# A streaming encoder layer with 16,384 product-key experts: sixteen more tokens by gathered rows, two gate blocks kept on chip

## The chip, the cores and the metric

The kernel runs on one core of one Trainium2 chip. Its time is the device time of one launch in microseconds, with the inputs in HBM. The core has five engines with instruction streams of their own: PE (TensorE, matmuls), DVE (VectorE), ACT (ScalarE), POOL (GpSimd) and SP (SyncE, which only issues DMAs here). They are ordered against one another by semaphores alone, which the kernel writes out by hand.

## The reference

One layer over 576 tokens (512 of a prompt, 64 of a decode step) with 1,024 channels: three attention-like branches, a merge, and then the part that the change touches, a feed-forward of single-neuron experts. For each token and each of 8 heads the 16 best of 16,384 experts are found by product keys (2 x 128 sub-keys); an expert is one row of `u` and one row of `v`, 1,024 numbers each.

```python
def peer_block(tok, wq, keys, u, v):
    qr = (tok @ wq).reshape(p, PEER_HEADS, 2, PEER_DQ // 2)
    s = jnp.einsum('phcd,hckd->phck', qr, keys)
    top_s, top_i = lax.top_k(s, PEER_TOPK)
    cand = top_s[:, :, 0, :, None] + top_s[:, :, 1, None, :]
    ...
    g = jax.nn.softmax(best, axis=-1)
    act = jax.nn.gelu(jnp.einsum('phkd,pd->phk', u[eidx], tok))
    return jnp.einsum('phk,phkd->pd', (g * act), v[eidx])
```

So each token needs 8 x 16 = 128 rows of `u` (a dot product with the token, then GELU), 128 shares `g`, and the sum of 128 rows of `v`, weighted by share times GELU. After that come the residual add and a final RMSNorm.

## The kernel before

**Two ways for the experts.** The last 128 tokens (`NSP`) go by gathered rows: partition p holds token p, POOL fetches for each of `NST` = 128 expert slots the 128 rows that the tokens need (one indirect DMA of 512 KB, `fetch`, L526), and DVE makes a dot product with the token (`dot`, L1408) or adds the weighted row to `accS` (`combine`, L1505). The first 448 tokens (`TD`) go densely: all 16,384 experts are computed for all of them, as `NCH` = 128 chunks of 128 experts, in two phases.

**Phase U.** For each chunk, PE multiplies the chunk of `u` with the tokens: 8 blocks of channels, each in three bf16 products (high x high, high x low, low x high), 24 matmuls of 448 columns (`chunk`, in `tile`, L1569). The weights come from HBM as f32 (SP, 512 KB, 4 buffers `raw`), ACT makes the high half (L581, a ring of 8) and POOL the low half (L493). ACT applies GELU into `hb` (2 buffers, L903) and stores it in HBM as `hd` (L906). Chunks are run in bodies of 8. Bodies 0 to 5 run beside DVE's search for the best experts (`top16`, `pairs_of`), during which DVE also makes the first 8 dot products: the first two stand between the second and third of five search parts. When the search is done ACT makes the exponentials (L944, ahead of chunk 40), DVE normalises them, makes 16 more dot products, and PE turns the triples (first key, second key, share).

**Gate steps.** In bodies 6 to 13 each chunk but the first of a body is followed by a gate step (`g_step`, L1930 and L1931): DVE makes one-hots of the two keys for 8 tokens (`one_hots`, L1470 to L1474, double-buffered), PE multiplies them (16 matmuls of 128 columns), and ACT copies the result, the share of each of the 16,384 experts for these 8 tokens, into `gsb` (L927). Seven steps are a block of 56 tokens (`TBLK`); two blocks fit `gsb`, and each is written to HBM as `gd` in 8 pieces (`write_piece`, L912) while the next is made. DVE makes 1.5 dot products a step. Bodies 14 and 15 have chunks only.

**Phase V.** For each chunk SP loads 4 chunks' gates `Gb` and activations `Hb` (896 KB each, double-buffered groups) and the chunk of `v`; DVE multiplies them into `wb` (L1519), ACT takes the high half `W_hi` (L954), DVE the low one (L1510) and also the low half of the `v` chunk (`unit_low`, L1486), and adds one gathered row slot (`combine`, L1505). PE makes 24 matmuls of 448 columns into the 8 banks of PSUM (`peer_v`, L1978; the last four chunks by channel block, L1997). Then the residual, the squares and the final norm. A phase V chunk starts on PE only when all GELUs (`gelu_done`), all dot products and its `W_lo` are done.

The order of each engine is that of its program. The ones that matter in what follows, for DVE in phase V:

```python
for c in range(NCH):
    # every 4th chunk: wait for Gb and Hb
    wb = Hb * Gb            # L1519
    unit_low(c + 2)         # L1486
    w_low(c - 1)            # L1510
    combine(c)              # L1505
```

and for ACT at the end of phase U, where `FIRST_W` is {5: (0,), 6: (1,), 7: (2, 3)}:

```python
for k in range(BODY):
    chunk(J_END + 1, k)     # GELU of this chunk, high half of the unit 8 ahead, store
    for c in FIRST_W.get(k, ()):
        w_high(c, c)        # waits for wb of chunk c
```

## Time and profile before

| what | value |
|---|---|
| time, median of 3 runs | 2072.77 us (2071.75 to 2074.18) |
| the profiled execution's own time | 2072.76 us |
| its span in the trace | 2071.0 us |
| mean granted TensorE clock | 0.988 of full |
| PE, DVE, ACT, POOL busy | 96%, 69%, 41%, 39% of the span |
| DMA | 467.12 MB, 226 GB/s over the span |
| phase U on PE | from about 826 to 1466 us |
| phase V on PE | from 1470 to about 2055 us |

The span is what the trace covers; the launch adds 1.8 us to it. A matmul's duration in the trace is from its start to the end of its pipeline, so two in a row overlap; what counts is the distance of their starts. A row of idle time in brackets says how long an engine stood still before an instruction and what released it.

### The profile page before, as it was taken

How to read it: one execution, taken by the hardware profiler on the slowest of the kernel's cores; microseconds unless marked ns; L12 is line 12 of the kernel's file. 1: busy time of each engine (PE TensorE's matmuls, PEld its weight loads, DVE VectorE, ACT ScalarE, POOL GpSimd, SP SyncE). 2: the span in 40 equal slices, each digit the busy share in tenths (PEclk: the TensorE clock that was granted, in tenths of full speed). 3: DMA queues.
4: the chain of work that ended last, by engine and by line, in shares of the span. 5: the costliest groups of instructions: out<-in, count | busy, mean ns of one | idle time of the engine just before them, and what ended most of it. 6: DMA issues, size and time to landing. Idle time of an engine off the chain costs nothing.

```text
span 2071.0 us, 34453 instructions
## 1 busy us (share of the span) xinstructions
PE 1997.3 (96%) x12670; PEld 1226.8 (59%) x12680; DVE 1434.0 (69%) x2704; ACT 841.4 (41%) x1253; POOL 807.7 (39%) x514
## 2 busy tenths in 40 slices
PE   7799998999999999999999999999999999999997
PEld 6546666677777777555555555555455555555554
DVE  7743645433345566989889898984788777777774
ACT  6324334344443433333346556653333333333331
POOL 2532211211233354565676667666332222222210
PEclk9899999999999999999999999999999999999998
DMA  5732112222344322466689999999999888899871
GB/s 190 183 107 85 51 41 86 75 70 80 137 143 130 102 73 72 161 214 215 234 320 322 357 355 359 356 353 400 384 362 371 330 329 327 329 342 340 328 264 46
DMA packets 180321, 467.12 MB, mean 226 GB/s; under 512 B 18600, under 2 KB 85168, under 8 KB 179448
## 3 DMA queue, kind: packets, MB, share of 16 engines
q1 hardware_dynamic: 102304, 248.84, 34.8%
q0 software_dynamic: 36864, 134.23, 17.5%
q10 hardware_dynamic: 41048, 82.66, 10.8%
q8 instruction: 64, 1.05, 0.2%
q14 instruction: 41, 0.34, 0.0%
HBM read 393.54 MB, written 72.14 MB: 225 GB/s over the span
## 4 chain that ended last, share of the span: by engine, by line
PE 81%; DVE 9%; DMA 4%; issue 2%; ACT 2%; POOL 1%; ACTq 0%; SPq 0%; DVEq 0%; POOLq 0%
PE ps L1569 29%; PE ps L1978 27%; PE ps L1661 10%; PE ps L1585 3%; PE ps L1808 2%; PE ps L1930 1%; POOL w_lo L493 1%; PE ps L1931 1%; DMA rows<-in_u_rows,rowi 1%; DVE rows L1408 1%; PE ps L1997 1%; DMA hd<-hb 1%; PE ps L1773 1%; PE ps L1788 1%; DMA raw<-in_units 1%
## 5 line engine op out<-in xcount | busy, mean ns | idle before, releaser
L493 POOL TENSOR_TENSOR w_lo<-raw,w_hi 128x1024 bf16<-128x1024 f32 x225 | 499.6, 2222 | 756.5 <-ACT w_hi L581 731.7
L581 ACT ACTIVATE w_hi<-raw 128x1024 bf16<-128x1024 f32 x357 | 374.9, 1052 | 481.0 <-PE ps L1978 302.0
L1569 PE MATMUL ps<-act_hi,w_hi 128*128 128x448 bf16 (+1 forms) x1040 | 364.1, 351 | 1.1 <-DVE proj L1034 0.7
L1569 PE MATMUL ps<-act_hi,w_lo 128*128 128x448 bf16 (+1 forms) x1040 | 364.2, 351 | 0.0
L1569 PE MATMUL ps<-act_lo,w_hi 128*128 128x448 bf16 (+1 forms) x1040 | 364.1, 351 | 0.0
L1978 PE MATMUL ps<-W_hi,w_hi 128*128 128x448 bf16 x992 | 350.7, 354 | 4.0 <-DVE W_lo L1510 4.0
L1978 PE MATMUL ps<-W_lo,w_hi 128*128 128x448 bf16 x992 | 350.6, 353 | 0.0
L1978 PE MATMUL ps<-W_hi,w_lo 128*128 128x448 bf16 x992 | 350.5, 353 | 0.0
L526 POOL DMA_INDIRECT rows<-in_v_units,rowi x128 | 149.4, 1167 | 415.2 <-DVE accS L1505 398.4
L1486 DVE TENSOR_TENSOR w_lo<-raw,w_hi 128x1024 bf16<-128x1024 f32 x128 | 156.6, 1223 | 116.6 <-ACT w_hi L581 116.6
L903 ACT ACTIVATE hb<-ps 128x448 f32<-128x448 f32 x128 | 69.7, 545 | 325.1 <-PE ps L1569 300.2
L1408 DVE CUSTOM_DVE_ANT_0 rows<-rows,ps 128x1024 f32<-128x1024 f32 x128 | 153.2, 1212 | 60.6 <-DMA rows<-in_u_rows,rowi 60.3
L1661 PE MATMUL ps<-act_hi,w_hi 128*128 128x288 bf16 x640 | 185.1, 289 | 7.5 <-ACT wk L712 3.5
L1661 PE MATMUL ps<-act_lo,w_hi 128*128 128x288 bf16 x640 | 185.0, 289 | 0.0
L1661 PE MATMUL ps<-act_hi,w_lo 128*128 128x288 bf16 x640 | 184.9, 289 | 0.0
L1505 DVE SCALAR_TENSOR_TENSOR accS<-rows,wsp,accS 128x1024 f32<-128x1024 f32 x128 | 163.5, 1277 | 0.0
L1569 PEld LDWEIGHTS ps<-act_hi,w_lo 128*128 128x128 bf16 x1040 | 101.7, 98 | 94.0
L1569 PEld LDWEIGHTS ps<-act_hi,w_hi 128*128 128x128 bf16 x1040 | 101.5, 98 | 90.4 <-issue 1.2
L1569 PEld LDWEIGHTS ps<-act_lo,w_hi 128*128 128x128 bf16 x1040 | 101.6, 98 | 88.4
L1978 PEld LDWEIGHTS ps<-W_hi,w_hi 128*128 128x128 bf16 x992 | 97.3, 98 | 95.5 <-issue 5.3
L1978 PEld LDWEIGHTS ps<-W_hi,w_lo 128*128 128x128 bf16 x992 | 97.3, 98 | 91.3 <-issue 1.1
L1978 PEld LDWEIGHTS ps<-W_lo,w_hi 128*128 128x128 bf16 x992 | 97.3, 98 | 91.0 <-issue 0.9
(374 smaller groups left out, 3323.2 us busy)
## 6 DMA issues: line engine op xcount, KB each, us to landing
raw<-in_u_units SPq DMA_DIRECT2D x128, 512.0 KB, 5.0
raw<-in_v_units SPq DMA_DIRECT2D x128, 512.0 KB, 9.4
raw<-in_units SPq DMA_DIRECT2D x100, 512.0 KB, 3.3
hd<-hb ACTq DMA_DIRECT2D x128, 224.0 KB, 5.4
...
```

The lines of the kernel that those rows point to most:

```text
L493: pool.tensor_tensor(w_lo[:, k % RING, :], raw[:, k % RAW, :], w_hi[:, k % RING, :], ALU.subtract).then_inc(lo_ready, 1)
L526: pool.indirect_dma_start(out=rows[:, s % RG, :], out_offset=None, in_=table, in_offset=bass.IndirectOffsetOnAxis(ap=rowi[:, s:s + 1], axi ...
L581: act.activation(w_hi[:, k % RING, :], raw[:, k % RAW, :], ACT.Copy).then_inc(hi_ready, 1)
L903: act.activation(hb[:, k % 2, :], ps[:, k % 2, 0:TD], ACT.Gelu_apprx_tanh).then_inc(gelu_done, 1)
L1408: dve.tensor_tensor_reduce(out=rows[:, s % RG, :], in0=rows[:, s % RG, :], in1=tok, scale=1.0, scalar=0.0, op0=ALU.mult, op1=ALU.add, accu ...
L1486: dve.tensor_tensor(w_lo[:, (U_V + c) % RING, :], raw[:, (U_V + c) % RAW, :], w_hi[:, (U_V + c) % RING, :], ALU.subtract).then_inc(lo_read ...
L1505: dve.scalar_tensor_tensor(out=accS[:, :], in0=rows[:, s % RG, :], scalar=wsp[:, s:s + 1], in1=accS[:, :], op0=ALU.mult, op1=ALU.add).then ...
L1569: last = pe.matmul(ps[:, bank + half, 0:n], w[:, slot, col:col + P], x(k)[:, half * n:(half + 1) * n], start=(k == 0 and w is w_hi and x i ...
L1585: last = pe.matmul(ps[0:nf, bank, :], x[:, k, f0:f0 + nf], w[:, n % RING, k2 * 512:(k2 + 1) * 512], start=(k == 0 and x is hi and w is w_h ...
L1661: last = pe.matmul(ps[:, 6 + half, 0:HALF], w[:, n % RING, k * P:(k + 1) * P], x[:, k, half * HALF:(half + 1) * HALF], start=(m == 0), sto ...
L1808: last = pe.matmul(ps[r0:r0 + rows, 4 + x % 2, 0:n], v, wk[0:ns, 2 + i % 2, b * P:b * P + n], start=(b == 0), stop=(b == len(blocks) - 1))
L1978: ins = pe.matmul(ps[:, d, 0:TD], w[:, slot, d * P:(d + 1) * P], x[:, k, :], start=(first and w is w_hi and x is W_hi), stop=False)
```

## The change

- **Tokens.** 16 of the 448 dense tokens (`NX`) leave the two dense phases: `TDX` = 432 columns a matmul, GELU on 432. They go by rows too. As they fill only 16 partitions, their 128 experts each are spread over 8 groups of 16 partitions: 16 slots, each an indirect DMA of 128 rows. Their gates are still made with the others (the gate steps and `W_hi`, `W_lo`, `wb` stay at 448 columns; the tail of `hb` is filled once).
- **Their token.** ACT copies the 16 tokens eight times over (`x_rep`), PE turns this in 8 transposes behind the first body, ACT copies it back from PSUM. Their row numbers and shares (`xpair`) are moved to the 8 groups by 8 small DMAs that POOL issues with chunks 100 to 107.
- **Their rows.** In phase V, DVE makes 16 more dot products (`x_dot`, behind chunks 4, 6, ... 34) and 16 more weighted additions (`x_combine`, behind chunks 72, 74, ... 102) into `accX`; ACT makes one small GELU ahead of chunk 64. POOL fetches in that order: 32 more indirect DMAs. At the end PE adds up the 8 groups by 8 small matmuls with `sel`, and DVE adds the result.
- **Gates.** Only 6 of the 8 blocks of gates are written to HBM and read back (`NBK`); the last two stay in `gsb`, and DVE's product is made by two instructions, one from `Gb`, one from `gsb`. Bodies 13 and 14 have no stores of gates.
- **Activations.** `hd` is laid out by groups of 4 chunks, so that a group's load has 7,168 bytes in a row for each partition, not 4 times 1,792.
- **Places.** As `gsb` is kept, `W_hi`, `W_lo`, `Gb0`, `Hb0` and `wb` lie where the tables of the gate steps were; `Gb1`, `Hb1` and `accS` lie in `act_hi` and `act_lo`, which PE reads until the end of phase U. So the load of group 1 and DVE's first `combine` wait for the last matmul of phase U (`unit_used, U_V`), and the load of group 0 for the last gate step. `accS` is no longer cleared: the first `combine` writes it.

```diff
@@ SP
             for b in range(2):
-                sp.wait_ge(b_written[b], NBLK // 2 * PIECES * 16)
+                sp.wait_ge(b_written[b], NBK // 2 * PIECES * 16)
+            sp.wait_ge(b_evac, N_STEP)
             for b in range(2):
                 sp.wait_ge(h_written[b], 8 * (NCH - 2 * GRP))
             load_gh(0, 0, None)
             for k in range(GRP, 2 * GRP):
                 load(a["v_units"][k], (U_V + k) % RAW, False, U_V + k - RAW + 1)
+            sp.wait_ge(unit_used, U_V)
             load_gh(1, 1, None)
@@ POOL
+                if LOADS_X <= c < LOADS_X + 2 * N_XG:
+                    half, g = divmod(c - LOADS_X, N_XG)
+                    pool.wait_ge(x_known, 2)
+                    at, to = half * HP + HP - NX, half * HP + g * NX
+                    pool.dma_start(xin[to:to + NX, :, :], xpair[at:at + NX, :, g * NX:(g + 1) * NX]).then_inc(x_moved, 16)
...
+            for c in range(NCH):
+                fetch_v(n_main(c), v_rows, rowi[:, c:c + 1])
+                i = (c - X_DOT) // 2
+                if c == X_DOT + 2 * i and 0 <= i < NX:
+                    fetch_v(n_dot(i), a["u_rows"], rowx[:, i:i + 1])
+                i = (c - X_COMB) // 2
+                if c == X_COMB + 2 * i and 0 <= i < NX:
+                    fetch_v(n_comb(i), v_rows, rowx[:, i:i + 1])
@@ ACT
-                        if b == 1:
+                        if b == 1 and not last:
                             write_piece(it * 2, 0, k, it * (2 * G_BODY) + G_BODY)
-                        elif not first:
+                        if b == 0 and not first:
                             write_piece(it * 2 - 1, 1, k, it * (2 * G_BODY))
...
             for k in range(BODY):
                 chunk(0, k, first=True)
+            act.wait_ge(x_turned, 1)
+            act.activation(x_rep[:, :], ps[:, 2:4, :].rearrange("p a b -> p (a b)"), ACT.Copy).then_inc(x_kept, 1)
@@ DVE
             def combine(s):
+                row = row_of(n_main(s))
                 if s:
...
+                else:
+                    dve.wait_ge(unit_used, U_V)
+                    dve.tensor_scalar(accS[:, :], row, wsp[:, 0:1], None, ALU.mult).then_inc(comb_done, 1)
+
+            def x_dot(s):
+                row = row_of(n_dot(s))
+                if s == 0:
+                    dve.wait_ge(x_kept, 2)
+                dve.tensor_tensor_reduce(out=row, in0=row, in1=x_rep[:, :], scale=1.0, scalar=0.0, op0=ALU.mult, op1=ALU.add,
+                                         accum_out=xtab[:, 0, s:s + 1]).then_inc(comb_done, 1)
...
-                dve.tensor_tensor(wb[:, c % 2, :].rearrange("p (b t) -> p b t", b=NBLK),
-                                  Hb[g % 2][:, k, :].rearrange("p (b t) -> p b t", b=NBLK),
-                                  Gb[g % 2][:, :, k, :], ALU.mult).then_inc(w_mul, 1)
+                dve.tensor_tensor(out[:, 0:NBK, :], h[:, 0:NBK, :], Gb[g % 2][:, :, k, :], ALU.mult)
+                dve.tensor_tensor(out[:, NBK:NBLK, :], h[:, NBK:NBLK, :], gsb[:, :, c, :], ALU.mult).then_inc(w_mul, 1)
...
                 combine(c)
+                i = (c - X_DOT) // 2
+                if c == X_DOT + 2 * i and 0 <= i < NX:
+                    x_dot(i)
+                i = (c - X_COMB) // 2
+                if c == X_COMB + 2 * i and 0 <= i < NX:
+                    x_combine(i)
@@ PE
-                tile((U_PEER + k) % RING, a_hi, a_lo, k % 2, n=TD, halves=1).then_inc(unit_used, 1)
+                tile((U_PEER + k) % RING, a_hi, a_lo, k % 2, n=TDX, halves=1).then_inc(unit_used, 1)
...
+            pe.wait_ge(x_kept, 1)
+            for x in range(KT):
+                last = pe.transpose(ps[:, 2 + x // 4, x % 4 * P:(x % 4 + 1) * P], x_rep[:, x * P:(x + 1) * P], ident[:, :])
+            last.then_inc(x_turned, 1)
...
-                        ins = pe.matmul(ps[:, d, 0:TD], w[:, slot, d * P:(d + 1) * P], x[:, k, :],
+                        ins = pe.matmul(ps[:, d, 0:TDX], w[:, slot, d * P:(d + 1) * P], x[:, k, 0:TDX],
```

## Rows read from the trace of the kernel before

**Rows 1.** The page: busy time of each engine; chain that ended last, by engine.

```profile
PE 1997.3 (96%) x12670; PEld 1226.8 (59%) x12680; DVE 1434.0 (69%) x2704; ACT 841.4 (41%) x1253; POOL 807.7 (39%) x514
...
PE 81%; DVE 9%; DMA 4%; issue 2%; ACT 2%; POOL 1%; ACTq 0%; SPq 0%; DVEq 0%; POOLq 0%
```

**Rows 2.** Busy by stage: us, PE, PEld, DVE, ACT, POOL, clock, DMA share, GB/s.

```profile
826.00:1045.00 219.00, 219.00 (x1163) 113.71 (x1163) 196.32 (x554) 75.61 (x103) 133.63 (x72) 1.00 0.62 212
1045.00:1094.00 49.00, 45.79 (x327) 26.24 (x326) 46.91 (x61) 25.48 (x24) 33.02 (x23) 1.00 0.83 299
1094.00:1393.20 299.20, 299.20 (x2131) 176.33 (x2129) 274.48 (x347) 180.00 (x161) 207.60 (x130) 1.00 0.97 352
...
1500.00:2000.00 500.00, 500.00 (x2645) 258.64 (x2644) 388.65 (x447) 170.00 (x223) 130.53 (x113) 1.00 0.91 339
```

**Rows 3.** Chain in order of time, gate steps: start us, us, what.

```profile
1104.07 4.54 PE ps L1569 x24
1109.53 4.54 PE ps L1569 x24
```

**Rows 4.** Timeline of PE, query projection: start us, us, instruction, [idle before].

```profile
788.53 0.42 PE L1569 MATMUL ps<-xg_hi,w_hi 128*128 128x288 bf16 x2
...
794.42 0.83 PE L1864 MATMUL ps<-keys,qr 128*128 128x128 f32 x6
```

**Rows 5.** Lines by form from 700 us: count | busy us, mean ns | idle.

```profile
L1569 PE MATMUL ps<-act_hi,w_hi 128*128 128x448 bf16 x1024 | 360.8, 352 | 0.3 <-ACT hb L903 0.3
L1978 PE MATMUL ps<-W_hi,w_hi 128*128 128x448 bf16 x992 | 350.7, 354 | 4.0 <-DVE W_lo L1510 4.0
...
L1947 PE MATMUL ps<-ident,proj 128*128 128x128 f32 x8 | 1.0, 273 | 0.0
```

**Rows 6.** Timeline of DVE ahead of the gate steps.

```profile
920.49 1.22 DVE L1408 CUSTOM_DVE_ANT_0 rows<-rows,ps 128x1024 f32<-128x1024 f32 x1 [3.98 <-DMA rows<-in_u_rows,rowi]
...
1010.50 2.18 DVE L1397 TENSOR_TENSOR trip<-best 128x64 f32<-128x64 f32 x1
...
1050.09 1.22 DVE L1408 CUSTOM_DVE_ANT_0 rows<-rows,ps 128x1024 f32<-128x1024 f32 x1 [0.17 <-DMA rows<-in_u_rows,rowi]
```

**Rows 7.** Timeline of ACT, softmax exponentials.

```profile
1012.72 1.52 ACT L944 ACTIVATE trip<-trip,rT 128x128 f32<-128x128 f32 x5 [1.07 <-DVE trip L1397]
```

**Rows 8.** Timeline of PE, first gate step.

```profile
1058.05 0.23 PE L1930 MATMUL ps<-hot_hi,hot 128*128 128x128 bf16 x1 [1.65 <-DVE hot_lo L1474]
```

**Rows 9.** Waits, gate steps, 1100 to 1400 us: us in total, times, longest.

```profile
DVE hot L1470 <- PE ps L1931: 17.7, 6, 3.7
DVE rows L1408 <- DMA rows<-in_u_rows,rowi: 12.0, 10, 4.0
```

**Rows 10.** Timeline of SP's queue, PE and DVE from phase U to phase V.

```profile
1462.78 3.26 SPq L439 DMA_DIRECT2D Hb<-hd  x1
...
1470.34 0.53 PE L1978 MATMUL ps<-W_hi,w_hi 128*128 128x448 bf16 x1 [3.97 <-DVE W_lo L1510]
...
1480.70 0.63 DVE L1519 TENSOR_TENSOR wb<-Hb,Gb 128x448 f32<-128x448 f32 x1 [6.68 <-DMA Hb<-hd]
```

**Rows 11.** Busy time of a stage of 5 us, columns as in rows 2.

```profile
1470.00:1475.00 5.00, 4.66 (x13) 1.90 (x14) 4.02 (x5) 2.01 (x4) 1.78 (x2) 0.50 1.06 396
```

**Rows 12.** Lines of DVE by form, 1500 to 2000 us.

```profile
L1505 DVE SCALAR_TENSOR_TENSOR accS<-rows,wsp,accS 128x1024 f32<-128x1024 f32 x112 | 143.1, 1277 | 0.0
L1486 DVE TENSOR_TENSOR w_lo<-raw,w_hi 128x1024 bf16<-128x1024 f32 x111 | 135.9, 1224 | 111.0 <-ACT w_hi L581 111.0
...
L1519 DVE TENSOR_TENSOR wb<-Hb,Gb 128x448 f32<-128x448 f32 x112 | 69.1, 617 | 0.0
```

**Rows 13.** DMA queues, 1500 to 2000 us: packets, MB, share of 16 engines.

```profile
q1 hardware_dynamic: 60175, 110.61, 60.8%
q0 software_dynamic: 16168, 58.89, 29.8%
```

**Rows 14.** DMA, 1400 to 1445 us: sum over the queues.

```profile
DMA packets 5804, 17.99 MB, mean 400 GB/s; under 512 B 644, under 2 KB 1789, under 8 KB 5802
```

More of the change, by code:

```diff
@@ L948, in _ @@
             two_bodies(0, first=True)
[L949 removed]
+            with act.Fori(1, NBK // 2) as it:
                 two_bodies(it)
+            two_bodies(NBK // 2, last=True)
             def w_high(c, slot):
@@ L2000, in _ @@
                 if d == 3:
-                    pe.wait_ge(comb_done, NST)
-                    pe.wait_ge(acc_done, 2)
+                    pe.wait_ge(comb_done, NST + 2 * NX)
+                    pe.wait_ge(x_sel, 1)
+                    pe.wait_ge(acc_done, 3)
+                    for e in range(KT):
+                        pe.matmul(ps[:, 2, e * NX:(e + 1) * NX], accX[:, e * P:(e + 1) * P], sel[:, :], start=True, stop=True)
                     for e in range(KT):
```

134 lines of the change are left out of this document (100 added, 34 removed).

## The prediction

> **What bounds the kernel now.** I read the page first. PE is busy for 96% of the span and holds 81% of the chain that ended last [rows 1]. So a shorter matmul pays, unless somebody else sets the pace in a stage; the busy time by stage says where to look. From 826 to 1045 us (bodies 0 to 5) PE never stands still, but DVE is busy for 196 of 219 us. From 1045 to 1094 us (body 6, the first gate steps) DVE is busy for 46.9 of 49 us, and this is the one stretch of phase U where PE has idle time, 3.2 us. From 1094 to 1393 us (bodies 7 to 13) and in phase V PE is full and DVE is not [rows 2].
>
> The chain in order of time shows what PE-bound looks like: 24 matmuls in 4.54 us, then a gate step, and the next chunk starts 5.46 us after the last [rows 3]. So a matmul of 448 columns takes 0.1892 us, a gate step 0.92 us, a body of eight chunks and seven steps 42.7 us.
>
> Then the waits of DVE ahead of the gate steps. Its second dot product waited 3.98 us for its rows, which POOL fetches at PE's pace. From there the search runs without a pause to 1012.7 us, and the sixteen dot products behind it end at 1051.3 us [rows 6]. ACT had already waited 1.07 us for the search when it ended [rows 7], and PE waited 1.65 us for the first one-hots [rows 8]. So PE and the search arrive together: a PE that arrives earlier waits.
>
> **The matmuls, removed columns.** In the query projection 24 pairs of 288 columns take 794.42 - 788.53 = 5.89 us [rows 4], 0.1227 us each. Between 288 and 448 columns a column costs 0.0665 / 160 = 0.416 ns, so 16 columns are 6.65 ns, and a chunk goes from 4.54 to 4.38 us, 0.16 us less. Phase U has 128 chunks (1,024 matmuls of each of three kinds), phase V as many (992 of each kind and the last four chunks) [rows 5]. If all counted, 2 x 20.4 = 41 us would go.
>
> **Phase U to 1094 us: most is given back.** 56 chunks save 9 us on PE. But DVE's chain has the same length and starts from PE's pace only once, at the fetch of the first rows, some 17 chunks in. PE is there 17 x 0.16 = 2.7 us earlier, less 0.9 us for the eight new transposes (as the eight of L1947, 1.0 us busy [rows 5]); these stand ahead of it. So the search ends 1.9 us earlier. ACT's exponentials stand ahead of GELU 40, so PE will wait there for some 2 us, and at the first gate step for some 6 us in place of 1.65. The bounds: nothing gained (0) and the whole 9 us; I take 1.9. DVE's new small operations (three of at most 128 columns) lie in front of dot products that wait for rows anyway, ACT's two copies of 1,024 columns in its idle time; without that cover they would cost DVE and ACT about 1 us each.
>
> **Bodies 7 to 15.** In bodies 7 to 13 a body falls to 8 x 4.38 + 7 x 0.92 = 41.5 us. DVE is busy for 274.5 of 299.2 us [rows 2], 39.2 us a body, and its waits were 12.0 us for rows and 17.7 us for PE in 300 us [rows 9], 1.7 and 2.5 us a body. The new body takes 1.2 us from the 2.5. So PE stays the bound by about 1 us a body: 7 x 8 x 0.16 = 9.0 us gained, of which I take off 1 us, as the DMAs then have to move 352 x 42.7 / 41.5 = 362 GB/s at a share that is already 0.97 [rows 2]. (Bounds: 0 off, and 5 off if DVE's waits double.) POOL's eight small loads cost it at most an indirect issue each, near 1 us, and it is busy for 208 of 299 us there. Bodies 14 and 15 have no gate steps: 16 x 0.16 = 2.6 us gained, and no stores of gates beside them any more.
>
> **The hand-over.** Now PE stands still for 3.97 us there [rows 10], and for 5 us behind it the granted clock is 0.50, its level of 1.2 GHz: 13 matmuls start where 26 would [rows 11], a loss of 2.5 us. The change moves work behind PE's last matmul of phase U. DVE's first `combine` now waits for it, and behind it in DVE's order stand the products of chunk 1, the low half of a unit, and only then `W_lo` of chunk 0, which PE needs: 1.28 + 0.62 (and up to 0.15 for the split) + 1.22 + 0.62 (`w_low` priced as the product, it has its 448 columns) = 3.8 us, by [rows 12], less about 0.07 us of overlap at each joint, 3.6 us. ACT's `W_hi` of chunk 1 waits for that product too, and the last GELU stands behind it; it is done by 3 us. So PE waits 3.6 us where it waited 3.97: 0.4 us gained, and the slow clock stays. SP's group 1 waits for PE's end as well: it is issued about 3.4 us behind it.
>
> **Phase V.** PE saves 128 x 0.16 = 20.4 us, if nobody else takes over. *DVE*: busy 388.7 us in 500 [rows 2], that is 110 chunks at 4.54 us, 3.53 us each. The split of the product costs at most 0.15 us: from 448 to 1,024 columns an instruction grows by 1224 - 617 = 607 ns, so 145 ns are left at none [rows 12]. An extra dot product (1.22 us [rows 6]) or addition (1.28 [rows 12]) on every second chunk is 0.64 us. Together 4.32 us, under 4.38: DVE just keeps up while the extras last, and has built no lead when the first come at chunk 4. *DMA*: a chunk with extras moves 0.524 MB of `v`, 1.5 x 0.524 of rows, 0.229 of `Hb` and 0.172 of `Gb`: 1.71 MB, in 4.38 us 391 GB/s. This holds for 62 chunks, 4 to 34 and 72 to 102. The others move 1.45 MB, 331 GB/s, no more than now. What the DMAs can do is bounded by two rows. Phase V now moves 339 GB/s at a share of 0.91 [rows 2, 13], which makes 372 at 1.00: 4.60 us a chunk, 0.22 x 62 = 14 us lost. And a stretch with mostly long packets moved 400 GB/s for 45 us [rows 14]: nothing lost. The new mix lies between (a quarter less of the 896-byte packets of `Gb`, and `Hb` in longer ones), so I take the middle, 386 GB/s, 4.44 us a chunk, 3 us lost.
>
> The Trainium skill (DMA: Bandwidth & Descriptors, Specifications) gives about 358 GB/s as the limit of HBM for one core. By that a chunk with extras takes 4.78 us, the extras cost 25 us, and the estimate would be 2065 us. The 400 GB/s of [rows 14] already exceed it, so I give it no more weight than the rival below has.
>
> **The end.** Eight more small matmuls for `accX`, at most as the eight transposes: 0.9 us more on PE. DVE's addition of 128 columns is hidden in its waits for PE.
>
> **Sum.** -1.9 - 9.0 + 1.0 - 2.6 - 0.4 - 20.4 + 3.0 + 0.9 = -29.4 us. The profiled execution took 2072.8 us, as did the median of the runs: 2043 us.
>
> **Rivals.**
> 1. *The DMAs bound the chunks with extras* at 372 GB/s: 14 us in place of 3, 2054 us. For it speaks the share of 0.91 now, and that DVE has no lead for the first stretch; against it that in the second stretch the rings of 8 give a lead, and [rows 14].
> 2. *The hand-over becomes a longer wait.* Group 1 was issued at 1462.8 us and its product began at 1480.7 us [rows 10], 17.9 us. Issued 3.4 us behind PE's end, with the same flight it comes at 21.3 us; `W_lo` of chunk 4 is ready 7 us later (4 and 5 of DVE's operations above, and the first extra dot product), at 28 us. PE wants it at 3.6 + 4 x 4.38 + 2.5 = 23.6 us, and may fall into the slow clock once more: 5 to 7 us lost, 2049 us. I expect a flight of about 9 us, as no stores of gates are in the way.
> 3. *Everything counts*: PE's 9 us ahead of 1094 us are kept and no DMA is in the way: 2032 us. Against it stands the busy DVE of 1045 to 1094 us.
> 4. *Slower.* The DMAs stay at the 339 GB/s that phase V moves now: 5.05 us a chunk, 0.67 x 62 = 42 us lost, 2082 us. This decides once a chunk with extras takes over 4.90 us (32.4 us of gain over 62 chunks), that is under 349 GB/s; [rows 14] speak against it.
> 5. *No fewer nanoseconds from fewer columns*: 2073 us. [rows 3, 4] speak against it.
>
> **Chances.** Forecast (2036 to 2048) 0.57; rival 1, 0.19; rival 2, 0.10; rival 3, 0.07; slower 0.04; nothing 0.03. From 2034 to 2060 us is what holds 8 in 10: it leaves out most of rival 3, the far end of rival 1 (the 2065 above) and the last two. A change of 0.2%, 4 us, is about the least that a measurement of this kernel can tell. Faster 0.92, the same 0.03, slower 0.05.
>
> **What would show it.** Chunks 4.38 us long in both phases; PE's first gate step behind an idle time near 6 us, and body 6 ending within 3 us of 1092; a body of 41.5 us from there; PE idle 3 to 5 us at the hand-over, no wait at chunk 4; in phase V, PE waiting for `W_lo` for a few us, all between chunks 4 and 40. It would be wrong if the waits of DVE for rows (L1505 and the extra dot product) passed 15 us, if PE waited at chunk 4, or if the gate steps showed PE waiting for one-hots in each body.

## The result and the profile after

The changed kernel takes 2039.19 us (median of four runs, 2037.23 to 2044.10), the kernel before 2073.41 us in the runs beside it: a ratio of 0.984, interval 0.982 to 0.986. The prediction said 2043. The profiled execution took 2040.82 us, 31.9 us less than before's; its span is 2038.6 us.

The page: busy time of each engine, then the chain that ended last.

```profile
PE 1963.5 (96%) x12694; PEld 1230.5 (60%) x12704; DVE 1463.6 (72%) x2885; ACT 847.1 (42%) x1257; POOL 892.6 (44%) x554
...
PE 76%; DVE 9%; DMA 6%; issue 4%; ACT 2%; POOL 2%; SPq 0%; ACTq 0%; DVEq 0%; POOLq 0%
```

Busy time by stage, columns as in [rows 2].

```profile
826.00:1045.00 219.00, 219.00 (x1219) 118.74 (x1218) 198.04 (x565) 79.02 (x110) 138.96 (x75) 1.00 0.63 220
1045.00:1094.00 49.00, 45.02 (x312) 26.93 (x310) 47.36 (x68) 26.30 (x25) 32.34 (x21) 0.93 0.78 281
1094.00:1393.20 299.20, 299.20 (x2179) 181.11 (x2177) 263.32 (x341) 184.27 (x167) 216.81 (x142) 1.00 0.97 353
...
1450.00:1500.00 50.00, 45.72 (x247) 23.81 (x248) 43.73 (x65) 14.45 (x20) 23.39 (x15) 1.00 0.91 344
1500.00:2000.00 500.00, 498.00 (x2722) 265.17 (x2721) 440.76 (x620) 178.32 (x230) 199.08 (x139) 1.00 0.92 354
```

PE's share has hardly moved, 34 us of work are gone. From 1094 us PE is full and DVE now waits more, 36 us in 299 where it was 25. In phase V DVE has risen from 389 to 441 us in 500 and PE still stands still for 2 us only. The new weak places are 1045 to 1094 us (4 us of idle time, clock 0.93) and 1450 to 1500 us (4.3 us).

DVE's lines by form, 1455 to 2022 us, against [rows 12]: the split product costs 502 + 269 ns, and the next instruction starts 0.61 us behind the first of the two; an extra dot product is 1.23 us, an extra addition 1.29.

```profile
L1591 DVE SCALAR_TENSOR_TENSOR accS<-rows,wsp,accS 128x1024 f32<-128x1024 f32 x126 | 161.2, 1279 | 0.0
L1565 DVE TENSOR_TENSOR w_lo<-raw,w_hi 128x1024 bf16<-128x1024 f32 x124 | 151.5, 1222 | 55.7 <-ACT w_hi L642 44.9 <-issue 10.8
...
L1630 DVE TENSOR_TENSOR wb<-Hb,Gb 128x336 f32<-128x336 f32 x125 | 62.8, 502 | 2.3 <-DMA Hb<-hd 2.3
L1631 DVE TENSOR_TENSOR wb<-Hb,gsb 128x112 f32<-128x112 f32 x125 | 33.7, 269 | 0.0
L1601 DVE CUSTOM_DVE_ANT_0 rows<-rows,x_rep 128x1024 f32<-128x1024 f32 x16 | 19.6, 1225 | 0.6
L1611 DVE SCALAR_TENSOR_TENSOR accX<-rows,xtab,accX 128x1024 f32<-128x1024 f32 x15 | 19.3, 1285 | 0.5
```

PE's timeline at the first gate step, the hand-over and the end (against [rows 8, 10]): the idle time is in brackets.

```profile
1053.93 0.29 PE L2048 MATMUL ps<-hot_hi,hot 128*128 128x128 bf16 x1 [3.98 <-DVE hot_lo L1553]
...
1449.07 0.35 PE L1687 MATMUL ps<-act_hi,w_lo 128*128 128x432 bf16 x1
1452.70 0.34 PE L2101 MATMUL ps<-W_hi,w_hi 128*128 128x432 bf16 x1 [3.29 <-DVE W_lo L1618]
...
2010.44 1.85 PE L2128 MATMUL ps<-sel,accX 128*128 128x16 f32 x16
2012.15 1.07 PE L2130 MATMUL ps<-ident,accS 128*128 128x128 f32 x8
```

DVE at the hand-over: the order is as predicted, the first combination (L1595) is 0.75 us, not 1.28: it writes `accS` and does not read it. From there it is 3.2 us to PE's start.

```profile
1449.52 0.75 DVE L1595 TENSOR_SCALAR accS<-rows,wsp 128x1024 f32<-128x1024 f32 x1 [7.68 <-PE ps L1687]
1450.19 0.50 DVE L1630 TENSOR_TENSOR wb<-Hb,Gb 128x336 f32<-128x336 f32 x1
1450.61 0.27 DVE L1631 TENSOR_TENSOR wb<-Hb,gsb 128x112 f32<-128x112 f32 x1
1450.80 1.22 DVE L1565 TENSOR_TENSOR w_lo<-raw,w_hi 128x1024 bf16<-128x1024 f32 x1
1451.93 0.62 DVE L1618 TENSOR_TENSOR W_lo<-wb,W_hi 128x448 bf16<-128x448 f32 x1
...
1463.04 0.51 DVE L1630 TENSOR_TENSOR wb<-Hb,Gb 128x336 f32<-128x336 f32 x1 [2.35 <-DMA Hb<-hd]
```

The last row is group 1's first product; SP issued its load at 1452.89 us, 10.2 us earlier, against 17.9 us before [rows 10].

Where the time went, from PE's timelines. "U" begins with the first chunk of phase U; each number is the distance from start to start, in us; "the squares' sum" is PE's first matmul of the final norm.

| stretch | before | after | gained | predicted |
|---|---|---|---|---|
| start of U to seventh gate step | 266.8 | 261.2 | 5.6 | |
| the same step by the clock of the trace (1092.98, 1088.06) | | | 4.9 | 1.9 |
| from there to the last matmul of U | 373.0 | 361.0 | 12.0 | 10.6 |
| hand-over | 4.33 | 3.63 | 0.7 | 0.4 |
| chunks 0 to 36 of phase V | 165.9 | 163.1 | 2.8 | |
| chunks 36 to 104 | 308.7 | 298.3 | 10.4 | |
| chunk 104 to the squares' sum | 112.3 | 110.2 | 2.1 | |
| all of phase V | 586.9 | 571.6 | 15.3 | 16.5 |

The changed kernel's phase U started 0.7 us later, hence 4.9 in place of 5.6. Behind the squares' sum it gives back another 1.0 us (0.5 in the rest of the norm, 0.5 outside the span).

### The profile page after: what moved, and what is told of

Its sections match the earlier page's. It is cut to its first block, busy times and chain, and to the rows that moved or that the text cites. A ratio compares the mean times of both kernels' runs of the same rounds, so it can differ in the third digit from the quotient of the medians.

```text
span 2038.6 us, 34629 instructions
## 1 busy us (share of the span) xinstructions
PE 1963.5 (96%) x12694; PEld 1230.5 (60%) x12704; DVE 1463.6 (72%) x2885; ACT 847.1 (42%) x1257; POOL 892.6 (44%) x554
## 4 chain that ended last, share of the span: by engine, by line
PE 76%; DVE 9%; DMA 6%; issue 4%; ACT 2%; POOL 2%; SPq 0%; ACTq 0%; DVEq 0%; POOLq 0%
PE ps L1687 32%; PE ps L2101 19%; PE ps L1779 10%; DMA raw<-in_v_units 4%; PE ps L1703 3%; PE ps L1926 2%; PE ps L2048 1%; PE ps L2049 1%; POOL w_lo L537 1%; ACT w_hi L642 1%; PE ps L1891 1%; PE ps L1906 1%; PE ps L2120 1%; DMA rows<-in_u_rows,rowi 1%; DVE eq L1470 1%
## 5 line engine op out<-in xcount | busy, mean ns | idle before, releaser
L1687 PE MATMUL ps<-act_hi,w_hi 128*128 128x432 bf16 (+1 forms) x1040 | 358.1, 346 | 0.7 <-DVE proj L1109 0.7
L1687 PE MATMUL ps<-act_hi,w_lo 128*128 128x432 bf16 (+1 forms) x1040 | 358.1, 346 | 0.0
L1687 PE MATMUL ps<-act_lo,w_hi 128*128 128x432 bf16 (+1 forms) x1040 | 358.1, 346 | 0.0
L2101 PE MATMUL ps<-W_hi,w_hi 128*128 128x432 bf16 x992 | 343.4, 346 | 6.9 <-DVE W_lo L1618 6.9
L2101 PE MATMUL ps<-W_hi,w_lo 128*128 128x432 bf16 x992 | 343.2, 346 | 0.0
L2101 PE MATMUL ps<-W_lo,w_hi 128*128 128x432 bf16 x992 | 343.2, 346 | 0.0
L570 POOL DMA_INDIRECT rows<-in_v_units,rowi x128 | 182.1, 1423 | 301.5 <-DVE accS L1591 280.7
L963 ACT ACTIVATE hb<-ps 128x432 f32<-128x432 f32 x128 | 67.9, 530 | 301.7 <-PE ps L1687 247.2
L1483 DVE CUSTOM_DVE_ANT_0 rows<-rows,ps 128x1024 f32<-128x1024 f32 x128 | 153.4, 1214 | 52.6 <-DMA rows<-in_u_rows,rowi 45.5
L2101 PEld LDWEIGHTS ps<-W_hi,w_hi 128*128 128x128 bf16 x992 | 97.0, 98 | 96.2 <-DVE W_lo L1618 8.0
L570 POOL DMA_INDIRECT rows<-in_u_rows,rowi x128 | 138.6, 1083 | 25.3 <-issue 15.7
```

What stands on the lines that cost most here:

```text
L570: pool.indirect_dma_start(out=rows[:, s % RG, :], out_offset=None, in_=table, in_offset=bass.IndirectOffsetOnAxis(ap=rowi[:, s:s + 1] if i ...
L963: act.activation(hb[:, k % 2, 0:TDX], ps[:, k % 2, 0:TDX], ACT.Gelu_apprx_tanh).then_inc(gelu_done, 1)
L1483: dve.tensor_tensor_reduce(out=rows[:, s % RG, :], in0=rows[:, s % RG, :], in1=tok, scale=1.0, scalar=0.0, op0=ALU.mult, op1=ALU.add, accu ...
L1687: last = pe.matmul(ps[:, bank + half, 0:n], w[:, slot, col:col + P], x(k)[:, half * n:(half + 1) * n], start=(k == 0 and w is w_hi and x i ...
L2101: ins = pe.matmul(ps[:, d, 0:TDX], w[:, slot, d * P:(d + 1) * P], x[:, k, 0:TDX], start=(first and w is w_hi and x is W_hi), stop=False)
```

## The experiments

Ratios are against the kernel before, run beside each; e1 to e4, e5 to e8, e9 and e10, e11 and e12 shared a chip each.

| run | median us | ratio (interval) |
|---|---|---|
| changed kernel | 2039.2 | 0.984 (0.982 to 0.986) |
| e1, 448 columns everywhere | 2073.1 | 1.000 (0.998 to 1.002) |
| e2, 448 columns in bodies 0 to 5 | 2044.6 | 0.986 (0.984 to 0.988) |
| e3, before with the new `hd` | 2072.6 | 1.000 (0.999 to 1.001) |
| e4, extra rows later | 2036.9 | 0.983 (0.981 to 0.984) |
| e5, first combination behind | 2035.8 | 0.983 (0.980 to 0.986) |
| e6, first gate wait filled | 2040.7 | 0.984 (0.982 to 0.987) |
| e7, extra dots without bytes | 2036.8 | 0.983 (0.980 to 0.986) |
| e8, extra dots without DVE time | 2041.6 | 0.984 (0.982 to 0.987) |
| e9, e4 and e5 together | 2032.5 | 0.980 (0.978 to 0.982) |
| e10, the changed kernel again | 2039.9 | 0.985 (0.982 to 0.987) |
| e11, before, `w_lo` in halves | 2069.1 | 0.998 (0.997 to 0.999) |
| e12, e9 with `w_lo` in halves | 2029.0 | 0.980 (0.978 to 0.981) |

And the stretches of their profiled executions, in us. "U begins" is the time of PE's first chunk of phase U, and the last column is the distance from there to the end of the span. "Exp." and "gate" are the distances from the same chunk to ACT's softmax exponentials and to the first gate step. "Search" is DVE from its second dot product to the softmax sums; "idle" is PE's at the hand-over. The three columns after it are chunks of phase V: 4, 32 and 36 chunks of 432 columns take 17.5, 140.2 and 157.7 us when PE never waits (18.2, 145.3 and 163.4 with 448). Chunks 72 to 104 took 140.2 us (145.3) in every kernel.

| kernel | U begins | search | exp. | gate | idle | 0-4 | 4-36 | 36-72 | U to end |
|---|---|---|---|---|---|---|---|---|---|
| before | 826.2 | 94.5 | 186.5 | 231.9 | 3.97 | 20.6 | 145.3 | 163.4 | 1244.8 |
| changed | 826.9 | 91.4 | 181.7 | 227.1 | 3.29 | 17.6 | 145.5 | 158.2 | 1211.8 |
| e1 | 832.4 | 96.1 | 187.4 | 232.7 | 3.28 | 19.8 | 145.3 | 163.4 | 1246.1 |
| e2 | 828.2 | 96.2 | 187.4 | 232.7 | 3.28 | 19.1 | 142.2 | 157.7 | 1215.7 |
| e3 | 828.5 | 95.2 | 186.5 | 231.8 | 3.25 | 19.8 | 145.3 | 163.4 | 1243.1 |
| e4 | 821.8 | 91.1 | 181.7 | 227.0 | 3.28 | 20.4 | 140.2 | 157.7 | 1209.2 |
| e5 | 828.4 | 92.1 | 181.7 | 226.9 | 1.22 | 17.5 | 142.4 | 157.8 | 1204.9 |
| e6 | 827.8 | 91.7 | 181.7 | 227.2 | 3.28 | 20.3 | 140.2 | 157.7 | 1209.4 |
| e7 | 830.3 | 91.0 | 181.8 | 227.1 | 3.28 | 18.1 | 140.2 | 157.7 | 1204.9 |
| e8 | 827.6 | 93.3 | 184.3 | 229.6 | 3.28 | 20.4 | 142.6 | 157.7 | 1214.1 |
| e9 | 827.5 | 92.1 | 181.7 | 226.9 | 1.63 | 17.5 | 140.2 | 157.7 | 1203.9 |
| e10 | 827.3 | 91.6 | 181.7 | 226.9 | 3.28 | 20.3 | 142.3 | 157.7 | 1210.4 |
| e11 | 825.1 | 93.5 | 185.5 | 231.8 | 4.11 | 19.8 | 145.3 | 163.4 | 1244.4 |
| e12 | 820.5 | 91.2 | 181.5 | 227.9 | 1.33 | 17.5 | 140.2 | 157.7 | 1203.9 |

Read the medians with the first column in mind: up to phase U all kernels but e11 and e12 do nearly the same work, and still they reach it anywhere from 821.8 (e4) to 832.4 us (e1). The last column is free of that.

**e1: all of the change but its columns.**

```diff
-tile((U_PEER + k) % RING, a_hi, a_lo, k % 2, n=TDX, halves=1)
+tile((U_PEER + k) % RING, a_hi, a_lo, k % 2, n=TD, halves=1)
-pe.matmul(ps[:, d, 0:TDX], w[...], x[:, k, 0:TDX], ...)   # both lines of peer_v
+pe.matmul(ps[:, d, 0:TD], w[...], x[:, k, :], ...)
```

> The changed kernel in all but its point: the matmuls of both phases keep 448 columns (the last 16 columns of the result are computed and not used). Theory A (the gain is the columns, nearly all else costs little): bodies 7 to 15 lose 72 x 0.16 = 11.5 us against the changed kernel, bodies 0 to 6 only the 2.7 us by which the first rows are fetched later, phase V 20.4 us less the 6 us that its first stretch with extras lost, as DVE then has 4.54 us a chunk; so 2039 + 29 = 2068 us, 5 us under the kernel before, chiefly the 2.4 us of slow clock at the hand-over. Theory B (the gates kept on chip and the longer packets are worth something by themselves, by DMAs that no longer delay ACT): 2060 us or less. Theory C (the extras cost more than all savings beside the columns): 2073 us or more.

2073.1 us: the columns make the whole gain, 34 us, and the rest of the change nets to nothing, within an interval of some 3 us either way. The 5 us that theory A gave it did not come: the clock fell behind the hand-over here (19.8 us for four chunks) and the end costs 1.8 us more than before's (114.1 against 112.3 us).

**e2: the columns kept at 448 in bodies 0 to 5 only.**

```diff
-def chunk(j, k, first=False):
+def chunk(j, k, first=False, n=TDX):
...
-    tile((U_PEER + k) % RING, a_hi, a_lo, k % 2, n=TDX, halves=1)
+    tile((U_PEER + k) % RING, a_hi, a_lo, k % 2, n=n, halves=1)
...
-    chunk(j, k)                          # bodies 0 to 5
+    chunk(j, k, n=TD)
```

> The changed kernel, with 448 columns in bodies 0 to 5 only (the 16 extra columns are computed and not used). Theory A (DVE's search, not PE, sets when the gate steps begin): PE arrives 48 x 0.16 = 7.7 us later, uses up the 4.0 us that it stood still ahead of the first gate step and the 2.3 us of slow clock behind it, and the search starts its second part up to 2.7 us later: the time grows by 1 to 3 us, to 2040 to 2042 us. Theory B (PE sets it, and the narrower matmul pays in bodies 0 to 5 as elsewhere): 7.7 us more, 2047 us.

2044.6 us, between the two theories. The early columns are worth 5.4 us in the medians and 6.1 us to the seventh gate step in the profiles (267.3 against 261.2), three times the predicted 1.9. The table says where: the exponentials, which wait for DVE's search, come 5.75 us later than in the changed kernel, and the search took 96.2 us where it takes 91.4 with 432 columns. So DVE's chain does not have "the same length".

**e3: the kernel before with `hd` by groups.** The store goes to `hd[group, :, k, :]` and the load reads 7,168 bytes in a row for each partition.

> The kernel before, with one part of the change alone: the activations stored by groups of four chunks, so that a load of a group has 7168 bytes in a row and not 4 x 1792. Theory A (phase V of the kernel before is bound by PE, so fewer packets change nothing): within 2 us of 2073, the DMA share of phase V falls from 0.91 by some hundredths. Theory B (the hand-over is late because of the DMAs, and shorter loads bring it forward): 2 to 5 us less, with PE standing still for less than 3.5 us and no slow clock behind it.

2072.6 us, no difference. The DMA share from 1500 to 2000 us is 0.90 where it was 0.91. The idle time at the hand-over is 3.25 us, under theory B's 3.5, but the clock still fell behind it (19.8 us for four chunks) and no time was won.

**e4: the extra rows begin later.**

```diff
-X_DOT, X_GELU, X_COMB = 4, 64, 72
+X_DOT, X_GELU, X_COMB = 36, 72, 96
```

> The changed kernel, with the extra dot products behind chunks 36 to 66 instead of 4 to 34, their GELU ahead of chunk 72 and the extra additions behind chunks 96 to 126. Theory A (the 5.9 us that phase V lost at chunks 4 to 36 come from DVE and the loads having no lead there; later on the rings of 8 have one): the loss goes, phase V's chunks take 4.38 us all through, 2034 us. Theory B (the DMAs cannot carry a gather more on every second chunk, wherever it is, when the dot products come): the loss moves to chunks 36 to 66 and the time stays at 2039 us.

2036.9 us. In the profile the 5.3 us lost in chunks 4 to 36 are gone, and of the later stretches none lost anything, though the 32 extra row DMAs had to be moved all the same. The median fell by only 2 to 3 us: the changed kernel does not always lose 5.3 there (e10: 2.1; e6, whose phase V is the same code: nothing), and e4's own profile has the slow clock behind the hand-over (20.4 us for four chunks).

**e5: the first combination behind the hand-over.**

```diff
-                combine(c)
+                if c == 1:
+                    combine(0)
+                if c:
+                    combine(c)
```

> The changed kernel, with DVE's first combine (the one that waits for PE's last matmul of phase U) moved behind the products of chunk 1, the low half of unit 3 and W_lo of chunk 0. Theory A (PE's 3.3 us of standing still at the hand-over are these operations queued behind the combine): PE stands still for about 1 us, for the last GELU alone, no slow clock follows; 2.3 us less, and 0 to 1.6 us more for the clock, 2035 to 2037 us. Theory B (ACT's last GELU waits for stores or loads, as in the kernel before, and the combine only hides it): 3 us or more as before, 2039 us.

2035.8 us. PE's timeline at the hand-over:

```profile
1450.81 0.35 PE L1690 MATMUL ps<-act_hi,w_lo 128*128 128x432 bf16 x1
1452.37 0.34 PE L2104 MATMUL ps<-W_hi,w_hi 128*128 128x432 bf16 x1 [1.22 <-issue]
```

2.1 us of idle time are gone and the clock stays at 1.00. The wait that remains is no longer for DVE; ACT's last GELU ended only 0.2 us before PE went on (1452.16 us).

**e6: 20 matmuls in the wait for the first one-hots.**

```diff
+                if first and s == 0:
+                    for x in range(20):
+                        pe.matmul(ps[:, 5, 0:TDX], act_hi[:, 0, 0:P], act_hi[:, x % KT, 0:TDX], start=True, stop=True)
                 pe.wait_ge(b_hot ...
```

> The changed kernel, with 20 more matmuls of 432 columns into a free bank of PSUM ahead of the first gate step (3.7 us of work whose result is not used), where PE stood still for 4.0 us. Theory A (the granted clock fell to 0.5 because of that idle time, and PE bounds body 6 from there): the first step to the second takes 5.3 us in place of 7.6, 2.3 us less, 2037 us. Theory B (DVE's one-hots bound body 6, as in the kernel before, so the slow clock cost nothing): 2039 us, with PE waiting for one-hots at later steps of body 6. Theory C (the clock falls all the same): 2039 us and 0.5 behind the first gate step.

2040.7 us. The clock stayed at 1.00, and PE waited for DVE three times more in body 6 instead. PE's waits from 1050 us on:

```profile
PE ps L2104 <- DVE W_lo L1618: 3.3, 1, 3.3
PE ps L2051 <- DVE hot_lo L1553: 2.2, 4, 0.6
```

So the slow clock at the first gate step, 2.3 us by the step from it to the next (7.65 us in the changed kernel, 5.31 here), costs nothing: DVE sets the pace of body 6.

**e7 and e8: the extra dot products' two costs apart.** e7 gathers 64 numbers a row in place of 1,024; e8 lets DVE multiply 16 columns of the full row.

```diff
-fetch_v(n_dot(i), a["u_rows"], rowx[:, i:i + 1])                                        # e7
+fetch_v(n_dot(i), a["u_rows"].rearrange("r (q w) -> (r q) w", w=64), rowx[:, i:i + 1], 64)
-dve.tensor_tensor_reduce(out=row, in0=row, in1=x_rep[:, :], ...                         # e8
+dve.tensor_tensor_reduce(out=row[:, 0:16], in0=row[:, 0:16], in1=x_rep[:, 0:16], ...
```

> The changed kernel, with the gathers for the 16 extra dot products cut to 64 numbers a row (256 bytes in place of 4096; the extra tokens' dot products are then made with wrong rows). DVE's work is unchanged. Theory A (the loads, at 391 GB/s asked, make the loss of 5.3 us at chunks 4 to 36): the loss goes, 2034 us. Theory B (DVE's 4.3 us a chunk without a lead make it): it stays, 2039 us.

> The changed kernel, with the 16 extra dot products cut to 16 columns (about 0.1 us each in place of 1.2; the extra tokens' dot products are then incomplete). The gathers are unchanged. Theory A (loads make the loss at chunks 4 to 36): it stays, 2039 us. Theory B (DVE makes it): it goes, 2034 us. If both this and the kernel without the bytes lose nothing, it takes both together.

Without the bytes nothing is lost in chunks 4 to 36; without DVE's time 2.4 us still are. One profile of each proves little, as e6 lost nothing there with bytes and DVE's time in place. All the profiles together do say it: of six kernels of 432 columns that fetch full extra rows from chunk 4 on, five lost 2.0 to 5.3 us (changed, e2, e5, e8, e10), and of four that fetch them later or short (e4, e7, e9, e12) none did. The changed kernel's own timeline around its first such wait shows the chain: ACT waits for the unit of `v`, DVE's low half of the unit for ACT, `W_lo` for its turn behind that, and PE for `W_lo`. (PE's losses come in a beat of four chunks, ahead of chunks 5 and 6, 9 and 10, 13 and 14. That is the beat of the groups, whose `Gb` and `Hb` pass through the same queue as the units.)

```profile
1472.63 1.06 ACT L642 ACTIVATE w_hi<-raw 128x1024 bf16<-128x1024 f32 x1 [3.55 <-DMA raw<-in_v_units]
...
1473.72 1.23 DVE L1565 TENSOR_TENSOR w_lo<-raw,w_hi 128x1024 bf16<-128x1024 f32 x1 [1.77 <-ACT w_hi L642]
1474.86 0.62 DVE L1618 TENSOR_TENSOR W_lo<-wb,W_hi 128x448 bf16<-128x448 f32 x1
...
1475.62 0.34 PE L2101 MATMUL ps<-W_hi,w_hi 128*128 128x432 bf16 x1 [0.79 <-DVE W_lo L1618]
```

**e9 and e10: both helpful edits together, and the changed kernel beside it.** The diffs are those of e4 and e5.

> The changed kernel with the two edits that helped alone: the first combination put behind the hand-over of the hi halves (e5), and the extra rows' stages begun at chunks 36, 72 and 96 in place of 4, 64 and 72 (e4). Theory A, the two gains add: they touch different waits. About 2.1 us of idle time goes at the hand-over and the clock does not fall behind it (0 to 2.4 us, by the changed kernel or by e4), and the 5.3 us at chunks 4 to 36 are not lost: 2031 to 2034 us, with no stretch of phase V's 32 chunks above 145.3 and 157.8 us. Theory B, they do not add: an earlier start of the gate steps' end takes the lead that the rows have, the loss comes back at chunks 36 to 72 or as waits in chunks 0 to 4, and the time is 2036 us or more.

> The changed kernel itself, on the same chip as e9. Both theories: 2037 to 2041 us. Its own profile tells how much of the time up to the first gate step (227.1 us from the last body's first chunk) and of chunks 4 to 36 (145.5 us) is the same from run to run: within 0.5 us if it is set by the code, up to 5 us apart if it is set by how the loads and the two engines happen to lie.

2032.5 against 2039.9 us: the gains add, 7.4 us (6.5 from U's start to the end in the profiles), and the profile of e9 has no loss in any stretch of phase V. The idle time is 1.63 us, 1.65 less than in e10 where 2.1 were expected, and the clock stays up. e10 repeats the changed kernel to 0.2 us from U's start to the first gate step, but splits its loss in chunks 0 to 36 otherwise: 2.8 us by the slow clock and 2.1 by loads, where the first profile had 0.1 and 5.3.

**e11 and e12: POOL's low half in two instructions**, on the kernel before and on e9.

```diff
-pool.tensor_tensor(w_lo[:, k % RING, :], raw[:, k % RAW, :], w_hi[:, k % RING, :], ALU.subtract).then_inc(lo_ready, 1)
+pool.tensor_tensor(w_lo[:, k % RING, 0:D // 2], raw[:, k % RAW, 0:D // 2], w_hi[:, k % RING, 0:D // 2], ALU.subtract)
+pool.tensor_tensor(w_lo[:, k % RING, D // 2:D], raw[:, k % RAW, D // 2:D], w_hi[:, k % RING, D // 2:D],
+                   ALU.subtract).then_inc(lo_ready, 1)
```

> The kernel before, with one edit: POOL makes each unit's low half (2.13 us alone) in two instructions of 512 columns instead of one of 1,024. Nothing is left out. The question is why DVE's search is 3 to 4 us shorter with 432 columns. Theory A: short instructions of DVE (the casts, 0.4 us alone, and the additions of 64 columns, 0.3 us alone) wait until the instruction that POOL has under way is over; with 448 columns the last six of them meet it (1.9 to 2.2 us each), with 432 they don't. With halves of some 1.1 us none of these six takes over 1.3 us, DVE's stretch from the second dot product to the softmax sums falls from 95.5 us by 3 us or more, the first gate step comes 2 to 3 us earlier, and the time is 2068 to 2071 us. Theory B: such an instruction runs beside POOL's at a lower speed whatever its length: the six stay at about 2 us, the search at 94 to 96 us, and the time within 2 us of 2072.

> The kernel of e9 (first combination behind the hand-over, extra rows later) with e11's edit. Theory A: there the search already passes POOL's instructions by, so at most 1 us is left to gain from the 1.9-us cast that remains: 2030 to 2033 us. Theory B: nothing, 2031 to 2034 us. POOL pays twice the start of an instruction, some 0.1 us a chunk, in its idle time (it is busy for 70% in bodies 7 to 13); if that is not hidden, PE waits for w_lo and the time is 2036 us or more.

Why look there: an addition of 128x64 numbers takes DVE 2.18 us in [rows 6] and 0.28 us in the changed kernel. POOL's timeline of the kernel before, at the same place (DVE's began at 1010.50 us and ended at 1012.68):

```profile
1010.43 2.13 POOL L493 TENSOR_TENSOR w_lo<-raw,w_hi 128x1024 bf16<-128x1024 f32 x1 [1.63 <-ACT w_hi L581]
```

DVE's instruction ends 0.1 us after POOL's. In the changed kernel POOL's ended before DVE's began (timelines of POOL and of DVE):

```profile
1005.56 2.12 POOL L537 TENSOR_TENSOR w_lo<-raw,w_hi 128x1024 bf16<-128x1024 f32 x1 [2.17 <-ACT w_hi L642]
...
1008.20 0.28 DVE L1472 TENSOR_TENSOR trip<-best 128x64 f32<-128x64 f32 x1
```

The last six short instructions of this kind in the search took 0.37, 2.19, 2.03, 2.20, 1.93, 2.18 us before, and 0.38 to 0.77 and 0.28 after. With halves (e11) they took 1.30, 1.25, 0.38, 1.23, 0.91 and 2.57 us: four of the five long ones are shorter, a short one rose to 1.30, and the last met both halves in a row. DVE's and POOL's timelines of e11:

```profile
1004.96 2.57 DVE L1399 TENSOR_TENSOR trip<-best 128x64 f32<-128x64 f32 x1
...
1005.11 1.17 POOL L493 TENSOR_TENSOR w_lo<-raw,w_hi 128x512 bf16<-128x512 f32 x1
1006.22 1.16 POOL L495 TENSOR_TENSOR w_lo<-raw,w_hi 128x512 bf16<-128x512 f32 x1
```

So the length of POOL's instruction sets how long DVE waits. But the waits are not simply gone where short instructions escape them: in the changed kernel the six took 8.3 us less than before and DVE's longer additions and products took 5.5 us more. One of them, a product that takes 1.23 us in before at the same place, is 3.08 us here beside POOL (timelines of DVE and of POOL):

```profile
1001.38 3.08 DVE L1468 TENSOR_TENSOR eq<-eq,topf 128x2048 bf16<-128x2048 bf16 x1
...
1001.26 2.12 POOL L537 TENSOR_TENSOR w_lo<-raw,w_hi 128x1024 bf16<-128x1024 f32 x1 [1.23 <-ACT w_hi L642]
```

e11's time fell to 2069.1 us, 3.5 us under before's and inside theory A's 2068 to 2071. The place that theory A named is not where it came from. The search did end 3.2 us sooner: 1.0 us by the table, and 2.19 us that DVE then waited for ACT.

```profile
1010.56 1.51 ACT L946 ACTIVATE trip<-trip,rT 128x128 f32<-128x128 f32 x5
...
1012.11 1.07 DVE L1437 TENSOR_REDUCE gs<-trip 128x32 f32<-128x512 f32 x1 [2.19 <-ACT trip L946]
```

But ACT's exponentials stand behind a GELU, so PE's chunks of 448 columns held them: they came 1.1 us earlier, the whole of the wait in [rows 7], and no more. From them to the first gate step POOL sets the pace, with a low half and two fetches of rows a chunk back to back. In halves such a round takes 4.65 us in place of 4.51, and the 1 us was lost again: 45.3 us from the exponentials to the first gate step in before, 46.3 in e11, and the first gate step as late as ever (231.8 against 231.9). From U's start to the end e11's profile took 1244.4 us, before's 1244.8 and e3's 1243.1.

The gain lies in an earlier stage, where the same edit holds. From 393 to 512 us PE waits for DVE to scale attention weights, and DVE for POOL: before, such an instruction takes 2.21 us from 408.86 us on, beside a low half of 2.12 us from 408.73 on, and its like in e11 takes 1.25 us beside a half of 1.15. PE's waits from 400 to 600 us and DVE's line from 393 us to the stage's end (512 and 510 us), before and then e11:

```profile
PE ps L1788 <- DVE wk L1276: 4.2, 4, 1.2
L1276 DVE TENSOR_SCALAR wk<-wk,st 128x384 f32<-128x384 f32 x6 | 7.9, 1317 | 0.2
```

```profile
PE ps L1790 <- DVE wk L1278: 1.0, 4, 0.3
L1278 DVE TENSOR_SCALAR wk<-wk,st 128x384 f32<-128x384 f32 x6 | 5.0, 832 | 0.2
```

PE takes 119.6 us for this stage (from its first `vpast` matmul to its first `mkT` matmul) in each of the twelve kernels with whole low halves, and 116.6 us in e11 and e12. That is 3.0 of the 3.5 us, in both pairs. So e11 landed in theory A's range by luck, with the mechanism right and the place wrong. e12 takes 2029.0 us, 3.5 us under e9 (on another chip), more than the 1 us that theory A allowed, and for the same reason: from U's start to the end e12 and e9 took 1203.9 us both. Of the 7.0 us between their profiles, 4.6 were there by 350 us already, which is the spread of the early stages.

## Why the prediction was right

The time came out 4 us under the forecast. Part of that closeness is luck: of the two largest misses, the forecast gave 3.0 us too little gain up to 1094 us and 2.9 us too little loss by the extra rows, and they cancel.

**The columns**, the largest term: 128 chunks at 4.38 us in place of 4.54 were predicted in each phase and are what the profiles show, to 0.1 us in 32 chunks. e1 shows that they alone make the gain.

**To 1094 us: the mis-sized term.** Predicted 1.9 us, found 4.9. Two things were right: PE's shorter chunks are partly given back at the first gate step, whose idle time rose from 1.65 to 3.98 us (6 were predicted), and the gate step comes earlier by as much as the search's end. The 2 us that PE was to wait at GELU 40 did not come (PE was busy for 219.00 of the 219 us up to 1045).

What failed is "DVE's chain has the same length and starts from PE's pace only once". The table shows it twice. The search is shorter with 432 columns in bodies 0 to 5 in every such profile (91.0 to 93.3 us against 94.5 to 96.2 for before, e1, e2 and e3). And its end does not follow its start: in six of the eight profiles with 432 columns throughout and whole low halves the second dot product began 91.9 to 92.9 us behind U's start, yet the exponentials came at 181.65 or 181.66 us in all six (181.8 in e7, 184.3 in e8). With 448 columns they came at 186.5 (before, e3) and 187.4 (e1, e2, which have the new transposes).

What ties the end to PE is POOL: its low halves follow PE's beat, one a chunk, and a DVE instruction that waits for one goes on when that one ends (in the changed kernel and in e5 the last long wait is for the low half that starts 174.4 us behind U's start). So the search takes up PE's pace again late in bodies 0 to 5, and the columns count there for more than the 17 chunks of the forecast: they bring the exponentials forward by 5.75 us (e2 against changed), as much as 36 chunks of 0.16 us, and the new transposes take 0.9 us of it back. [rows 6] showed the wait unread: 2.18 us for 64 columns stands beside rows of 1.22 us for 1,024. Which of DVE's instructions meets a low half is chance of the beat; why e8 ended 2.6 us later than the others is open.

Behind the exponentials nothing more is gained, for DVE's dot products wait for rows, and POOL fetches these at its own pace, 4.51 us a chunk where PE now needs 4.38:

```profile
1022.10 2.13 POOL L537 TENSOR_TENSOR w_lo<-raw,w_hi 128x1024 bf16<-128x1024 f32 x1
...
1026.59 2.15 POOL L537 TENSOR_TENSOR w_lo<-raw,w_hi 128x1024 bf16<-128x1024 f32 x1
```

From the exponentials to the first gate step it is 45.2 to 45.5 us in all twelve kernels with whole low halves, whatever their columns.

The Trainium skill (SBUF — State Buffer, Who interferes with whom) says that a DVE instruction with two inputs in SBUF, or a cast in a two-port mode, contends with a GpSimd instruction that reads SBUF, and that the later one blocks until the earlier is over. By that rule, the trace agrees: 1010.50 + 2.18 against 1010.43 + 2.13. The 2.57 us of e11 agree less well: by the records DVE's instruction began 0.15 us ahead of POOL's first half and still ended 0.15 us behind the second.

**Bodies 7 to 15.** Predicted 10.6 us, found 12.0. A body takes 41.46 us, as predicted. The 1 us taken off for the DMAs was not lost (PE's 299.20 of 299.20 us), and a wait of before's at 1443.49 us, 0.5 us by the starts, went. DVE's waits, 1094 to 1378 us, against [rows 9]:

```profile
DVE hot L1549 <- PE ps L2049: 19.0, 7, 4.1
...
DVE rows L1483 <- DMA rows<-in_u_rows,rowi: 6.0, 8, 1.4
```

The waits for rows halved; rival 3's "no DMA is in the way" was right about this part.

**The hand-over.** Idle 3.29 us, predicted 3.6, for the reason given: DVE's order. Two prices were off, the first combination (0.75, not 1.28 us) and the split (0.61 us from the product's start to the next instruction's where before's has 0.54, 0.07 more and not up to 0.15). "The slow clock stays" was wrong in the first profile and right in e10, though the idle times are equal to 0.01 us. Windows of 3 us of the changed kernel behind the hand-over (columns as in [rows 2]), then of e4, whose code up to there is the same:

```profile
1453.00:1456.00 3.00, 3.00 (x19) 1.58 (x17) 3.00 (x6) 0.00 (x0) 1.98 (x1) 1.00 0.96 362
1456.00:1459.00 3.00, 3.00 (x18) 1.65 (x17) 3.00 (x6) 1.99 (x3) 2.35 (x2) 1.00 1.09 372
```

```profile
1447.00:1450.00 3.00, 1.98 (x6) 0.87 (x7) 3.00 (x6) 0.23 (x1) 0.66 (x1) 0.53 0.76 220
1450.00:1453.00 3.00, 3.00 (x9) 1.18 (x8) 3.00 (x5) 1.23 (x2) 2.35 (x2) 0.50 1.04 378
```

18 or 19 matmuls fall into 3 us at 1.00 (2.4 GHz), 9 at 0.50 (1.2 GHz).

**Group 1 (rival 2)** did not come: its flight was 10.2 us, near the 9 expected, and PE did not wait at chunk 4.

**Extra rows.** Predicted 3 us lost over both stretches; the first profile lost 5.9, e10 2.1, e5 2.3, e6 nothing, and none of them anything in chunks 72 to 104. Windows of the changed kernel over chunks 4 to 36 and 72 to 104:

```profile
1470.00:1616.00 146.00, 142.73 (x773) 74.12 (x771) 132.27 (x194) 49.62 (x64) 67.94 (x49) 1.00 0.97 375
...
1774.00:1914.00 140.00, 140.00 (x769) 75.07 (x768) 129.40 (x174) 51.23 (x64) 67.28 (x46) 1.00 1.00 384
```

384 GB/s at a share of 1.00 is the estimate of 386 almost exactly; but as a term, rate times 62 chunks was the wrong form. The second stretch runs at that limit and loses nothing; that full rings cover the missing 2% is the likely reason. The first one has no lead. e4, e7, e9 and e12 lose nothing there once the extras have a lead or no bytes. What keeping two gate blocks on chip is worth beside the extras was not run: with their bytes the first stretch would ask for 404 GB/s (1.77 MB in 4.38 us), an estimate from the prediction's own bytes. The slow clock and the loads together cost 5.4 us (changed), 5.3 (e8), 4.9 (e10), 3.6 (e2), 2.8 (e6) and 2.2 (e5). A PE held up by the clock may give the loads their lead; that is argued and not shown, and e5, which lost nothing by the clock and only 2.2 by the loads, does not fit it.

The Trainium skill (HBM Reference, Specifications (TRN2)) says that a core which streams alone measures well above the 358 GB/s that the prediction weighed. The trace agrees: 384 GB/s over 140 us.

**The end.** 1.7 us for the small matmuls (2010.44 to 2012.15), predicted 0.9: the eight f32 matmuls of 16 columns stand as 16 in their row, 0.107 us each, and so take twice the eight transposes by which they were priced (0.90 us from 2012.15 us on). e1 has the same with 1.8.

**The sum.** Predicted -29.4; found in the profiles: to 1094 us -4.9, bodies 7 to 15 -12.0, hand-over -0.7, no slow clock behind it -2.4, columns of phase V -20.4, extras +5.9, end +1.7, unexplained +1.0: -31.8 (by the times -31.9; the rest is rounding). The misses have both signs, of 3 us each at most.
